# The first unit behind a norm in two narrow halves, one of them ahead of the norm's last turn; next weights requested earlier behind the mixers; a signal of their own for the convolution's taps

## The chip, the cores and the metric

The kernel runs on one core of one Trainium2 chip. The metric is the device time of one execution in microseconds. PE is the engine of the matrix products (TensorE), DVE is VectorE, ACT is ScalarE, POOL is GpSimd and SP is the engine that issues most of the DMAs (SyncE); SPq is SP's DMA issuing as the trace shows it. Kernels are compared by the median of runs that alternate on the same chip.

## What is computed

Two models in a row, batch 1, 512 tokens, width 1024, all in fp32. Their parts, cut to what matters here:

```python
def swiglu(h, w1, w3, w2):
    return (jax.nn.silu(h @ w1) * (h @ w3)) @ w2          # width of the hidden layer: 2816

def post_norm_residual(x, y, gate, weight, g, b):
    return layer_norm(ALPHA * x + weight * (1.0 + gate) * y, g, b)

def first_block(x, ...):                                   # 2 layers
    for l in range(DEPTH):
        h = x * (1.0 + scale[:, 0]) + shift[:, 0]
        x = post_norm_residual(x, swiglu(h, ...), gate[:, 0], 0.5, ...)
        h = x * (1.0 + scale[:, 1]) + shift[:, 1]
        x = post_norm_residual(x, hybrid_mixer(h, ...), gate[:, 1], 1.0, ...)
        h = x * (1.0 + scale[:, 2]) + shift[:, 2]
        x = post_norm_residual(x, swiglu(h, ...), gate[:, 2], 0.5, ...)

def hybrid_layer(x, ...):                                  # second model, 2 layers
    proj = rms_norm(x, norm1_g) @ w_in
    qkv = jax.nn.silu(causal_depthwise_conv(qkv, dn_conv_w))    # taps: 4 x 1536
    ...
    x = x + jnp.concatenate([o_dn, o_sc], axis=-1) @ w_out
    h2 = rms_norm(x, norm2_g)
    x = x + (jax.nn.silu(h2 @ ffn_w_gate) * (h2 @ ffn_w_up)) @ ffn_w_down
```

Every product of this program is a product of the normed and transposed h with a weight matrix that is read once from HBM.

## The kernel before

**Products.** An fp32 number is held as a high part (rounded to fp32r) and a low part (the rest). `product` (L159) makes one fp32 product of three matmuls: high x high (L163), low x high (L164), high x low (L165). Each matmul has a weight load of its own (PEld). ACT casts a weight to its high part, and DVE subtracts that from the weight to get the low part (`low_part`, L168). The weights come by DMA into two slots of `m_raw`. A "unit" is one tile of 128 output features over all 512 tokens: 8 slices k of the width 1024, 24 matmuls of 128x512. A 512-token tensor has 4 tiles of 128 tokens (TT is 4, DT is 8, HALF is 4).

**Stages.** The program is a row of stages, each opened by `stage` (L125), with a barrier of all engines between them (the profile names it by branches at L130). First model, twice: ffn0, proj1 and its attention stages, out1, ffn2. Second model, twice: proj2, delta, out2, ffn3. A stage's name ends in its layer: out1_0 is the output product of the first layer's mixer.

**The end of a stage with a norm.** `Down` (L494) makes the last product of an ffn or a mixer with the tokens on the partitions, 4 tiles in 8 banks of PSUM, row block by row block (`load_rows`, `high_act`, `low_dve`, `products`). While the last four row blocks are done tile by tile (`last_pe`, L572), ACT and DVE norm each finished tile (`norm_act` L627, `norm_dve` L721), PE turns the normed tile into columns (`turn_pe`, L593), and ACT and DVE make high and low parts of the turned tile (`high_norm`, `low_norm`). The norm of the last tile has nothing to hide behind but `keep_running` (L173): matmuls of a constant into an unused bank, which compute nothing. `filled` (L511) tells how many: 5 times two in a layer norm ("ln"), 3 times two in an rms norm ("rms"), and 7, with 12 more a tile earlier, where both follow each other ("ln_rms", the seam between the models).

**The start of the next stage.** `Ahead` (L103) requests the two first weight chunks of the next stage from the end of this one: ffn and mixer stages by `ahead.load(sp)`. `first_high_act` and `first_low_dve` (L110 to L116) split one slice k of the first chunk, 128x256, into `m_first_high` and `m_first_low` at the head of the norm. The next stage's PE starts with k = 0 on these, and goes on as the other 7 slices, 256 columns each, are split (`first_high`, `first_low`, L1107 to L1115, for the projections; the loops at the head of the scalar and vector blocks of `ffn`). The high and low parts of the second half (k of 4 and over) of the last tile are made in the next stage too: `carry_high` and `carry_low` (L480 to L490). In ffn, the two products of block f = 0 are made side by side, k by k.

**out1 and out2** (`mix_out`, L2215). 8 row blocks; SP requests blocks 4 to 7, waits until all 8 are split, and only then requests both slots of the next stage's weights. Everything of the norm waits for these weights, as the split stands at its head:

```python
            if ahead is not None:
                sp.wait_ge(S.rows_split, down.n)
                ahead.load(sp)
```

**proj2** (`mixer2_project`, L2344). POOL requests 11 small vectors, 4 of them the convolution's taps, all on one signal. DVE's first convolution step (L2373) waits for all 11, and behind it in DVE's order stands the low part of weight chunk 2.

**ffn's vectors.** `load_vectors` requests gate, shift, scale or gain ahead of the down product's rows, into room of their own.

Of the kernel before, what the change touches and what calls it, by code (L numbers as in the profile page):

```python
# [17 lines left out]
F32R = mybir.dt.float32r  # L18
# [80 lines left out]
class Memory:  # L99
    pass  # L100


class Ahead:  # L103


    def __init__(self, nc, tag, load, slots=2, first=None, count=0):
        self.landed = [nc.alloc_semaphore(f"{tag}_ahead{s}") for s in range(slots)]
        self.load = lambda sp: load(sp, self.landed)
        self.first, self.count = first, count

    def first_high_act(self, act, M):
        act.wait_ge(self.landed[0], self.count)
        high, _, raw = self.first(M)
        return act.copy(high, raw)

    def first_low_dve(self, dve, M):  # L116
        high, low, raw = self.first(M)
        return low_part(dve, low, raw, high)
# [375 lines left out]
class Down:  # L494
# [4 lines left out]
    def __init__(self, nc, memory, tag, M, I, boundary, w_down, raw, rows_high, rows_low, following, gate=None, gate_there=False, extra=0):  # L499
# [9 lines left out]
        self.vec = [sb(f"vec{n}", D) for n in range({"ln": 2, "ln_rms": 3, "rms": 1, "final": 1}[boundary.kind])]  # L509

        self.filled = {"ln": {TT - 1: 5}, "rms": {TT - 1: 3}, "ln_rms": {TT - 2: 12, TT - 1: 7}, "final": {}}[boundary.kind]  # L511
# [4 lines left out]
    def load_vectors(self, sp, S, gate_free=False):  # L516

        M, I, b = self.M, self.I, self.boundary
        if gate_free:
            sp.wait_ge(S.residual, 3 * TT)  # L520
        row = lambda ap: ap.partition_broadcast(P)
        if b.kind in ("ln", "ln_rms") and not self.gate_there:
            sp.dma_start(self.gate[:], row(M.mod_dram[b.layer, b.sub, 2])).then_inc(S.gate_landed, 16)
# [69 lines left out]
    def turn_pe(self, pe, S, i):  # L593
# [252 lines left out]
def ffn_first(M):  # L846
    two = lambda w: w[:].rearrange("p (w n) -> p w n", w=2)
    return two(M.first_high), two(M.first_low), M.raw[:, 0].rearrange("p (w k n) -> p w k n", w=2, k=DT)[:, :, 0]


def ffn_ahead(nc, M, tag, w_gate, w_up):
    return Ahead(nc, tag, lambda sp, landed: [ffn_load(sp, M, landed, w_gate, w_up, s, s) for s in range(2)], first=ffn_first, count=32)


def ffn(nc, M, I, tag, w_gate, w_up, w_down, boundary, mine, ahead=None, ada=None, residual=None, hid=None, carried=True):
# [5 lines left out]
    with ExitStack() as memory, stage(nc, tag, signals, mine) as (block, S):  # L861
# [9 lines left out]
                    ahead, res.g if res else None)  # L871
        down.rows_landed = [S.rows0_landed, S.rows1_landed, S.rows2_landed]
        down.ht = hid[:, 0:2 * TT, :].rearrange("p (i c) n -> p i (c n)", i=TT)
        done_first = 1 if carried else 0
# [7 lines left out]
        def _(sp):  # L882
            if res:
                res.load(sp, S)
            for f in range(2, FT):
                if f == 2:
                    sp.wait_ge(S.first_split, DT - done_first)
# [5 lines left out]
            down.load_vectors(sp, S, res is not None)  # L893
# [5 lines left out]
            for f in range(3, FT):  # L899
                down.load_rows(sp, S, f)  # L900
# [2188 lines left out]
```

## Time and profile before

| | us |
|---|---|
| median of 3 runs | 3656.82 (3651.94 to 3661.17) |
| the profiled execution's own time | 3657.5 |
| its span | 3655.7 |
| busy PE / DVE / ACT / POOL | 3561.3 / 1975.7 / 1227.5 / 150.9 |
| mean granted TensorE clock | 0.993 of full speed |

The profile is one execution on its one core. Its page gives the busy time of each engine; the timeline gives the start and length of each instruction, or of a group of equal ones, and in brackets the idle time before it with what ended it; the windows view gives busy time and the granted clock (PEclk, 1.00 is 2.4 GHz, 0.50 is 1.2 GHz) of a stretch. Matmuls are pipelined: a matmul of 128x512 lasts 0.39 us but the next starts after some 0.23 us, so the pace is read from the distance of starts. L numbers are lines of the kernel before.

### The profile page before, as it was taken

The page shows a single profiled execution, that of the slowest core. Times are in us where ns is not written, and L with a number is a line of the kernel's source. Part 1 is how long each engine was busy: PE and PEld are TensorE (multiplying, and loading weights), DVE is VectorE, ACT ScalarE, POOL GpSimd, SP SyncE. Part 2 cuts the span into 40 slices and gives each one's busy share as a digit, 9 for nine tenths or more (in the row PEclk, how much of TensorE's full clock was granted, in tenths as well). Part 3 has the DMA queues.
Part 4 walks back from the last instruction along what each step waited for, and adds up shares of the span by engine and source line. Part 5 has one row for each costly group of instructions (what it writes and reads, how often), then busy time and mean ns, then how long its engine had stood idle before and what let it go on. Part 6 is the DMA issues. An engine that isn't in the chain of part 4 may idle for free. (4 is left out here: it accounts for less than half of the span.)

```text
span 3655.7 us, 43309 instructions
## 1 busy us (share of the span) xinstructions
PE 3561.3 (97%) x17744; PEld 2933.0 (80%) x17744; DVE 1975.7 (54%) x3041; ACT 1227.5 (34%) x1928; POOL 150.9 (4%) x212
## 2 busy tenths in 40 slices
PE   7999999999999999999999999999999999999999
PEld 6888777678888888777678887788788878878887
DVE  6555665775456645665663355666322366553233
ACT  3222334532233222334532223635322355442222
POOL 1110100001000100100000001000000000000000
PEclk8999999999999999999999999999999999999999
DMA  7654331245433644331144331211334222113322
GB/s 268 230 184 128 83 102 41 71 154 190 143 128 110 219 161 128 83 96 47 55 131 126 106 136 48 79 38 53 92 94 126 98 48 75 41 53 104 104 98 81
DMA packets 438041, 397.74 MB, mean 109 GB/s; under 512 B 53779, under 2 KB 390275, under 8 KB 437844
## 3 DMA queue, kind: packets, MB, share of 16 engines
q1 hardware_dynamic: 413028, 310.53, 27.9%
q0 software_dynamic: 24816, 84.45, 6.8%
q8 instruction: 140, 2.29, 0.3%
q14 instruction: 57, 0.47, 0.0%
HBM read 390.14 MB, written 4.78 MB: 108 GB/s over the span
## 5 line engine op out<-in xcount | busy, mean ns | idle before, releaser
L163 PE MATMUL m_ps<-m_h_high,ffn_w_high 128*128 128x512 f32 x2100 | 821.7, 391 | 1.0 <-DVE ffn_w_low L170 1.0
L165 PE MATMUL m_ps<-m_h_high,ffn_w_low 128*128 128x512 f32 x2100 | 818.0, 390 | 0.0
L164 PE MATMUL m_ps<-m_h_low,ffn_w_high 128*128 128x512 f32 x2100 | 817.6, 389 | 0.0
L163 PEld LDWEIGHTS m_ps<-m_h_high,ffn_w_high 128*128 128x128 f32 x2100 | 394.8, 188 | 82.6 <-issue 1.1
L165 PEld LDWEIGHTS m_ps<-m_h_high,ffn_w_low 128*128 128x128 f32 x2100 | 394.5, 188 | 82.8
L164 PEld LDWEIGHTS m_ps<-m_h_low,ffn_w_high 128*128 128x128 f32 x2100 | 394.8, 188 | 81.3
L971 ACT ACTIVATE ffn_sil<-m_ps 128x512 f32<-128x512 f32 x132 | 79.1, 599 | 1128.9 <-PE m_ps L165 1128.9
L163 PE MATMUL m_ps<-ffn_w_high,ffn_hid_high 128*128 128x512 f32 x1056 | 411.6, 390 | 0.0
L165 PE MATMUL m_ps<-ffn_w_high,ffn_hid_low 128*128 128x512 f32 x1056 | 410.9, 389 | 0.0
L164 PE MATMUL m_ps<-ffn_w_low,ffn_hid_high 128*128 128x512 f32 x1056 | 410.9, 389 | 0.0
L1011 DVE TENSOR_TENSOR ffn_hid<-ffn_sil,m_ps 128x512 f32<-128x512 f32 x110 | 75.6, 687 | 549.7 <-ACT ffn_sil L971 549.6
L170 DVE TENSOR_TENSOR ffn_w_low<-m_raw,ffn_w_high 128x2048 fp32r<-128x2048 f32 (+1 forms) x168 | 303.7, 1823 | 112.4 <-ACT ffn_w_high L965 108.7
L170 DVE TENSOR_TENSOR ffn_w_low<-ffn_rows,ffn_w_high 128x1024 fp32r<-128x1024 f32 x132 | 161.6, 1224 | 291.5 <-ACT ffn_hid_high L979 291.4
L556 ACT CAST ffn_w_high<-ffn_rows 128x1024 fp32r<-128x1024 f32 x132 | 138.5, 1049 | 407.9 <-PE m_ps L165 395.4
L965 ACT CAST ffn_w_high<-m_raw 128x2048 fp32r<-128x2048 f32 x126 | 239.7, 1902 | 0.3 <-DMA m_raw<-in_ffn_w 0.2
L165 PEld LDWEIGHTS m_ps<-ffn_w_high,ffn_hid_low 128*128 128x128 f32 x1056 | 198.2, 188 | 41.2
L163 PEld LDWEIGHTS m_ps<-ffn_w_high,ffn_hid_high 128*128 128x128 f32 x1056 | 198.3, 188 | 41.1
L164 PEld LDWEIGHTS m_ps<-ffn_w_low,ffn_hid_high 128*128 128x128 f32 x1056 | 198.3, 188 | 40.5
L394 DVE SCALAR_TENSOR_TENSOR ffn_ada_part<-ffn_rows,m_ccol,ffn_ada_part 128x512 f32<-128x512 f32 x224 | 168.2, 751 | 86.8 <-DMA ffn_rows<-in_ada_w 78.8
L380 POOL DMA_DIRECT2D ffn_rows<-in_ada_w x128 | 91.2, 713 | 1475.0 <-issue 885.7
L163 PE MATMUL m_ps<-m_h_high,proj_w_high 128*128 128x512 f32 (+2 forms) x344 | 142.6, 415 | 3.5 <-DVE proj_w_low L170 3.5
L1535 ACT ACTIVATE attn_probs<-attn_probs,attn_shift 128x128 f32<-128x128 f32 (+3 forms) x128 | 71.0, 556 | 193.6 <-DVE attn_shift L1590 193.5
(485 smaller groups left out, 5439.3 us busy)
## 6 DMA issues: line engine op xcount, KB each, us to landing
m_raw<-in_ffn_w SPq DMA_DIRECT2D x176, 512.0 KB, 4.7
ffn_rows<-in_ada_w POOLq DMA_DIRECT2D x128, 512.0 KB, 5.0
ffn_rows<-in_ffn_w SPq DMA_DIRECT2D x88, 512.0 KB, 3.5
m_raw<-in_w_in SPq DMA_DIRECT2D x32, 1024.0 KB, 5.3
m_raw<-in_ffn_w_gate SPq DMA_DIRECT2D x44, 512.0 KB, 3.7
m_raw<-in_ffn_w_up SPq DMA_DIRECT2D x44, 512.0 KB, 4.8
ffn_rows<-in_ffn_w_down SPq DMA_DIRECT2D x44, 512.0 KB, 3.7
m_raw<-in_w_out SPq DMA_DIRECT2D x24, 512.0 KB, 4.7
```

What stands on the lines that cost most here:

```text
L163: pe.matmul(out, sh, mh, start=first, stop=False, skip_group_check=True)
L164: pe.matmul(out, sh, ml, start=False, stop=False, skip_group_check=True)
L165: return pe.matmul(out, sl, mh, start=False, stop=last, skip_group_check=True)
L170: return dve.tensor_tensor(low, value, high.bitcast(F32), ALU.subtract)
L380: queue.dma_start(self.slots[:, n % 2], src).then_inc([S.ada0_landed, S.ada1_landed][n % 2], 16)
L394: dve.scalar_tensor_tensor(out=part, in0=self.slots[:, n % 2, j, :], scalar=self.M.ccol[:, k + j:k + j + 1], in1=part, op0=ALU.mult, op1=A ...
L556: return act.copy(self.high[f % self.SLOTS], self.raw[f % self.raws])
L965: act.copy(w_high[:, f % 2], M.raw[:, f % 2]).then_inc(S.wide_high, 1)
L971: act.activation(sil[:, f % 2, :], M.ps[:, 2 * (f % 2), :], ACT.Silu).then_inc(S.silu_done, 1)
L1011: dve.tensor_tensor(hid[:, f, :], sil[:, f % 2, :], M.ps[:, 2 * (f % 2) + 1, :], ALU.mult).then_inc(S.hidden_done, 1)
L1535: ins = act.activation(probs(m, g), probs(m, g), ACT.Exp, bias=shift[:, m % 4, g:g + 1], accum_out=sums[:, p % 4, g, b:b + 1])
```

## The change

There are nine ends of a norm with a stage behind them: ffn0_0, out1_0, ffn2_0, ffn0_1, out1_1, ffn2_1, out2_0, ffn3_0 and out2_1. At each of them:

1. At the head of the norm, ACT and DVE split the whole first unit of the next stage (128 columns, all 8 slices k: 128x1024 each) into a new buffer `M.early`, where one slice of 256 columns was split before.
2. PE makes the first unit in two halves of 256 tokens (`half_pe`, 24 matmuls of 128x256 each). Half 0, of tokens 0 to 255, stands ahead of the last tile's turn, in place of that turn's `keep_running`. Half 1 is the next stage's first work. The 12 fillers of "ln_rms" a tile earlier stay.
3. The next stage begins with the carried parts of h on ACT and DVE, and splits the second 128 columns of chunk 0 in two pieces of four k. In ffn, bank 0 is now finished before bank 1 begins. ffn0_0, which has no norm ahead of it, makes both halves at its start, after its own split of 128x1024.

Further: 4. in `mix_out`, slot 0 of the next weights is requested once 6 of 8 row blocks are split, and slot 1 after 8. 5. In proj2, the 4 tap requests have a signal of their own; the first convolution step waits for them alone, and the others are waited for at a step much later (`gain`, n = 0). 6. In ffn, the gate is requested where all vectors were, and the rest behind row block 18 into spent rows of the hidden layer, which frees the room that `M.early` takes.

```diff
     def first_high_act(self, act, M):
         act.wait_ge(self.landed[0], self.count)
-        high, _, raw = self.first(M)
-        return act.copy(high, raw)
+        return act.copy(M.early[:, 0], self.first(M))
...
+    def half_pe(self, pe, M, half, S=None):
+
+        tokens = slice(2 * P * half, 2 * P * (half + 1))
+        for k in range(DT):
+            if S and k == HALF:
+                pe.wait_ge(S.carry_low, 2)
+            mm = product(pe, M.ps[:, 0, tokens], (M.early[:, 0, k], M.early[:, 1, k]), (M.h_high[:, k, tokens], M.h_low[:, k, tokens]),
+                         k == 0, k == DT - 1)
+        return mm
...
-        self.filled = {"ln": {TT - 1: 5}, "rms": {TT - 1: 3}, "ln_rms": {TT - 2: 12, TT - 1: 7}, "final": {}}[boundary.kind]
+        self.filled = {TT - 2: 12} if boundary.kind == "ln_rms" else {}
...
         if self.filled.get(i):
             pe.wait_ge(S.h_low, 1)
             keep_running(pe, self.M, 0, self.filled[i])
+        if i == TT - 1:
+            pe.wait_ge(S.next_low, 1)
+            pe.wait_ge(S.h_low, 2)
+            self.following.half_pe(pe, self.M, 0)
         pe.wait_ge(S.h_ready, i + 1)
...
             for f in range(3, FT):
                 down.load_rows(sp, S, f)
+                if f == SPENT_ROW:
+                    sp.wait_ge(S.rows_split, SPENT)
+                    down.load_vectors(sp, S)
...
                 if f == 0:
+                    if not carried:
+                        pe.wait_ge(S.first_split, 1)
+                        mine.half_pe(pe, M, 0)
+                    mine.half_pe(pe, M, 1, S if carried else None)
                     for k in range(DT):
-                        if k >= done_first:
-                            pe.wait_ge(S.first_split, k + 1 - done_first)
-                        if k == HALF and carried:
-                            pe.wait_ge(S.carry_low, 2)
-                        for which in range(2):
-                            w = (ffn_first(M)[0][:, which], ffn_first(M)[1][:, which]) if k == 0 else (high[:, which, k], low[:, which, k])
-                            mm = product(pe, bank(which), w, (M.h_high[:, k, :], M.h_low[:, k, :]), k == 0, k == DT - 1)
+                        if k % HALF == 0:
+                            pe.wait_ge(S.first_split, own_first + 1 + k // HALF)
+                        mm = product(pe, bank(1), (high[:, 1, k], low[:, 1, k]), (M.h_high[:, k, :], M.h_low[:, k, :]), k == 0, k == DT - 1)
...
-            if ahead is not None:
-                sp.wait_ge(S.rows_split, down.n)
-                ahead.load(sp)
+            for s in range(2):
+                sp.wait_ge(S.rows_split, down.n - 2 + 2 * s)
+                ahead.load(sp, s)
...
             if u == 0:
-                dve.wait_ge(S.others_landed, 16 * len(others))
+                dve.wait_ge(S.taps_landed, 16 * len(taps))
...
     def gain(n):
         def step(dve, S, link):
             half, i = n // TT, n % TT
+            if n == 0:
+                dve.wait_ge(S.others_landed, 16 * len(others))
```

How the instructions stand on PE at the end of ffn0_0 and the start of proj1_0, before (`m_tri,m_ident` are the fillers, L605 the turns):

```order
L605 MATMUL m_ps<-m_ident,m_hid 128x128 x7
L176 MATMUL m_ps<-m_tri,m_ident 128x256 [waits ffn0_0_h_low]
L176 MATMUL m_ps<-m_tri,m_ident 128x256 x4
L605 MATMUL m_ps<-m_ident,m_hid 128x128 [waits ffn0_0_h_ready]
L605 MATMUL m_ps<-m_ident,m_hid 128x128 x3
...
L1178 UNCONDITIONAL_BRANCH [waits barrier_Pool_Activation_PE_DVE_SP_release]
L163 MATMUL m_ps<-m_h_high,m_first_high 128x512
L164 MATMUL m_ps<-m_h_low,m_first_high 128x512
L165 MATMUL m_ps<-m_h_high,m_first_low 128x512
L163 MATMUL m_ps<-m_h_high,proj_0_w_high 128x512 [waits proj1_0_first_split]
```

And now:

```order
L624 MATMUL m_ps<-m_ident,m_hid 128x128 x7
L175 MATMUL m_ps<-m_h_high,m_early_first 128x256 [waits ffn0_0_h_low,ffn0_0_next_low]
L176 MATMUL m_ps<-m_h_low,m_early_first 128x256
L177 MATMUL m_ps<-m_h_high,m_early_first 128x256
...
L624 MATMUL m_ps<-m_ident,m_hid 128x128 [waits ffn0_0_h_ready]
L624 MATMUL m_ps<-m_ident,m_hid 128x128 x3
...
L1202 UNCONDITIONAL_BRANCH [waits barrier_Pool_Activation_PE_DVE_SP_release]
L175 MATMUL m_ps<-m_h_high,m_early_first 128x256
...
L175 MATMUL m_ps<-m_h_high,m_early_first 128x256 [waits proj1_0_carry_low]
...
L175 MATMUL m_ps<-m_h_high,proj_0_w_high 128x512 [waits proj1_0_first_split]
```

The fillers are gone. 24 matmuls of the next stage stand in their place, with waits for the split and for two low parts of the turned tile before; 24 more stand behind the barrier, 12 of them ahead of the wait for the carried low part, and the first wait for a piece of the new split comes after them all.

DVE at the start of proj1_0, before:

```order
L1215 UNCONDITIONAL_BRANCH [waits barrier_Pool_Activation_PE_DVE_SP_release]
L170 TENSOR_TENSOR proj_0_w_low<-m_raw,proj_0_w_high 128x256 [waits proj1_0_first_high] x3
L170 TENSOR_TENSOR m_h_low<-m_ps,m_h_high 128x4x128
L170 TENSOR_TENSOR m_h_low<-m_ps,m_h_high 128x4x128 [waits proj1_0_carry_high]
L170 TENSOR_TENSOR proj_0_w_low<-m_raw,proj_0_w_high 128x256 [waits proj1_0_first_high] x4
L170 TENSOR_TENSOR proj_0_w_low<-m_raw,proj_0_w_high 128x8x28 [waits proj1_0_w_high]
```

And now:

```order
L1239 UNCONDITIONAL_BRANCH [waits barrier_Pool_Activation_PE_DVE_SP_release]
L182 TENSOR_TENSOR m_h_low<-m_ps,m_h_high 128x4x128
L182 TENSOR_TENSOR m_h_low<-m_ps,m_h_high 128x4x128 [waits proj1_0_carry_high]
L182 TENSOR_TENSOR proj_0_w_low<-m_raw,proj_0_w_high 128x4x128 [waits proj1_0_first_high] x2
L182 TENSOR_TENSOR proj_0_w_low<-m_raw,proj_0_w_high 128x8x28 [waits proj1_0_w_high]
```

Seven pieces of the first chunk became two of half its width in all, and the carried low parts stand ahead of them.

## Rows read from the trace of the kernel before

**Rows 1.** The page: busy time of each engine over the span

```profile
PE 3561.3 (97%) x17744; PEld 2933.0 (80%) x17744; DVE 1975.7 (54%) x3041; ACT 1227.5 (34%) x1928; POOL 150.9 (4%) x212
```

**Rows 2.** Window view (columns: window, length, busy of each engine, PEclk, DMA share, GB/s)

```profile
776.00:1134.00 358.00, 357.11 (x1606) 296.52 (x1607) 196.06 (x214) 92.39 (x101) 22.81 (x32) 1.00 0.46 152
```

**Rows 3.** Timeline (start, us, engine, line, operation), norm at the end of ffn0_0

```profile
423.87 1.23 DVE L170 TENSOR_TENSOR m_h_low<-m_ps,m_h_high 128x1024 fp32r<-128x1024 f32 x1
...
426.23 2.32 PE L176 MATMUL m_ps<-m_tri,m_ident 128*128 128x256 f32 x10
...
429.30 0.42 PEld L605 LDWEIGHTS m_ps<-m_ident,m_hid 128*128 128x128 f32 x4 [1.15 <-DVE m_hid L757]
```

**Rows 4.** Timeline, wide and narrow products on PE, and a weight load

```profile
1163.54 0.39 PE L163 MATMUL m_ps<-m_h_high,ffn_w_high 128*128 128x512 f32 x1
...
1174.42 0.39 PE L163 MATMUL m_ps<-m_h_high,ffn_w_high 128*128 128x512 f32 x1
...
2345.08 0.28 PE L165 MATMUL m_ps<-proj_w_high,m_h_low 128*128 128x256 f32 x1
...
2345.44 0.19 PEld L163 LDWEIGHTS m_ps<-proj_w_high,m_h_high 128*128 128x128 f32 x1
...
2347.59 0.28 PE L165 MATMUL m_ps<-proj_w_high,m_h_low 128*128 128x256 f32 x1
```

**Rows 5.** Timeline, PE at the end of ffn3_0's norm (rms)

```profile
2955.15 1.46 PE L176 MATMUL m_ps<-m_tri,m_ident 128*128 128x256 f32 x6
...
2957.48 0.42 PEld L605 LDWEIGHTS m_ps<-m_ident,ffn_hid 128*128 128x128 f32 x4 [1.27 <-DVE ffn_hid L760]
```

**Rows 6.** Timeline, PE at the start of proj2_0

```profile
2261.97 0.40 PE L165 MATMUL m_ps<-m_h_high,m_first_low 128*128 128x512 f32 x1
...
2262.66 0.40 PE L164 MATMUL m_ps<-m_h_low,proj_w_high 128*128 128x512 f32 x1
```

**Rows 7.** Timeline, the split in front of ffn0_0's norm, and a cast of 1024

```profile
405.38 0.42 DVE L170 TENSOR_TENSOR m_first_low<-m_raw,m_first_high 128x256 fp32r<-128x256 f32 x1
...
407.54 1.22 DVE L709 CUSTOM_DVE_ANT_0 m_xr<-m_ps,m_xr 128x1024 f32<-128x1024 f32 x1 [1.74 <-PE m_ps L165]
...
745.97 1.05 ACT L556 CAST out_w_high<-m_raw 128x1024 fp32r<-128x1024 f32 x1 [4.39 <-PE m_ps L165]
```

**Rows 8.** Timeline, out1_0 from the sixth row's split to the first turn

```profile
737.07 1.22 DVE L170 TENSOR_TENSOR out_w_low<-m_raw,out_w_high 128x1024 fp32r<-128x1024 f32 x1
...
747.05 1.23 DVE L170 TENSOR_TENSOR out_w_low<-m_raw,out_w_high 128x1024 fp32r<-128x1024 f32 x1 [4.21 <-ACT out_w_high L556]
748.30 3.78 SPq L843 DMA_DIRECT2D m_raw<-in_ffn_w  x4
...
753.59 0.41 ACT L114 CAST m_first_high<-m_raw 128x256 fp32r<-128x256 f32 x1 [6.58 <-DMA m_raw<-in_ffn_w]
...
757.73 0.39 PE L165 MATMUL m_ps<-out_w_high,m_h_low 128*128 128x512 f32 x1
...
759.91 0.48 PE L163 MATMUL m_ps<-out_w_high,m_h_high 128*128 128x512 f32 x1
```

**Rows 9.** Timeline and one window, start of proj2_0

```profile
2263.18 4.05 POOL L1167 DMA_DIRECT2D b_conv_w<-in_dn_conv_w  x4 [244.37 <-issue]
...
2278.10 0.09 DVE L2373 MEMSET b_raw<- 128x36 f32 x1 [9.83 <-DMA b_norm_g<-in_dn_norm_g]
...
2284.73 2.28 DVE L170 TENSOR_TENSOR proj_w_low<-m_raw,proj_w_high 128x2048 fp32r<-128x2048 f32 x1
...
2287.07 0.28 PEld L163 LDWEIGHTS m_ps<-m_h_high,proj_w_high 128*128 128x128 f32 x1 [3.17 <-DVE proj_w_low L170]
...
2283.40:2305.00 21.60, 19.25 (x73) 14.39 (x72) 18.56 (x23) 12.74 (x15) 0.00 (x0) 0.92 0.32 98
```

**Rows 10.** Timeline at the start of ffn0_0, and a window in proj1_1

```profile
49.07 0.29 PEld L163 LDWEIGHTS m_ps<-m_h_high,m_first_high 128*128 128x128 f32 x1 [7.17 <-DVE m_first_low L170]
...
1529.00:1533.00 4.00, 4.00 (x12) 2.96 (x12) 3.82 (x10) 2.74 (x9) 0.00 (x0) 0.57 0.01 4
```

More of the change, by code:

```diff
@@ L846, in ffn_first @@
 def ffn_first(M):
-    two = lambda w: w[:].rearrange("p (w n) -> p w n", w=2)
-    return two(M.first_high), two(M.first_low), M.raw[:, 0].rearrange("p (w k n) -> p w k n", w=2, k=DT)[:, :, 0]
+    return M.raw[:, 0].rearrange("p (w k n) -> p w k n", w=2, k=DT)[:, 0]
+SPENT, SPENT_ROW = 14, 18
 def ffn_ahead(nc, M, tag, w_gate, w_up):
-    return Ahead(nc, tag, lambda sp, landed: [ffn_load(sp, M, landed, w_gate, w_up, s, s) for s in range(2)], first=ffn_first, count=32)
+    return Ahead(nc, tag, lambda sp, landed, *slots: [ffn_load(sp, M, landed, w_gate, w_up, s, s) for s in slots or range(2)], first=ffn_first, count=32)
 def ffn(nc, M, I, tag, w_gate, w_up, w_down, boundary, mine, ahead=None, ada=None, residual=None, hid=None, carried=True):
@@ L983, in _ @@
                 mine.first_high_act(act, M).then_inc(S.first_high, 1)
-            for k in range(1, DT):
-                if k == HALF and carried:
-                    carry_high(act, S, M)
-                act.copy(view(w_high, 0)[:, :, k], M.raw[:, 0].rearrange("p (w k n) -> p w k n", w=2, k=DT)[:, :, k]).then_inc(S.first_high, 1)
+            else:
+                carry_high(act, S, M)
+            for ks in first_pieces:
+                act.copy(view(w_high, 0)[:, 1, ks], view(M.raw, 0)[:, 1, ks]).then_inc(S.first_high, 1)
             split(1)
@@ L1027, in _ @@
                 mine.first_low_dve(dve, M).then_inc(S.first_split, 1)
-            for k in range(1, DT):
-                if k == HALF and carried:
-                    carry_low(dve, S, M)
-                dve.wait_ge(S.first_high, k + 1 - done_first)
-                low_part(dve, view(w_low, 0)[:, :, k], M.raw[:, 0].rearrange("p (w k n) -> p w k n", w=2, k=DT)[:, :, k],
-                         view(w_high, 0)[:, :, k]).then_inc(S.first_split, 1)
+            else:
+                carry_low(dve, S, M)
+            for n, ks in enumerate(first_pieces):
+                dve.wait_ge(S.first_high, own_first + n + 1)
+                low_part(dve, view(w_low, 0)[:, 1, ks], view(M.raw, 0)[:, 1, ks], view(w_high, 0)[:, 1, ks]).then_inc(S.first_split, 1)
             split(1)
@@ L1165, in _ @@
                     res.load(pool, S)
+                for dst, src in taps:
+                    pool.dma_start(dst, src).then_inc(S.taps_landed, 16)
                 for dst, src in others:
@@ L2487, in mixer2_project @@
     pe_steps.update({U + 2: turn_steps})
[L2488 removed]
+    project(nc, M, I, f"proj2_{l}", mixer2_chunks(I.w_in_2[l]), tiles, taps=taps, others=others, late_others=late_others, mine=mine, ahead=ahead,
             dve_steps=dve_steps, act_steps=act_steps, pe_steps=pe_steps, banks=4,
```

86 lines of the change are left out of this document (47 added, 39 removed).

## The prediction

> **What bounds the kernel now.** I read the page first: PE is busy for 3561.3 of 3655.7 us [rows 1]. Then the windows view inside an ffn: between 776 and 1134 PE is busy for 357.11 of 358.00 us at a clock of 1.00 [rows 2]. So neither DMA nor DVE sets the time there; only less work on PE, or an idle stretch of it filled, can move the end. Then the timeline of PE where the stages meet, since PE's busy time also holds work that serves nothing. At the end of ffn0_0 the last wide product is followed by turns, then ten filler matmuls from 426.23, and the last tile's turn starts at 429.30, when DVE has normed it [rows 3]. These 3.07 us are a latency of ACT and DVE, and the fillers only occupy PE. The change puts real work there at nine such seams.
>
> The sum is made against the profiled execution's own 3657.5 us, which lies 0.7 above the median of 3656.8.
>
> **Half units at nine seams.** The reader sees the price of a wide matmul in the distance of two starts: 48 matmuls of 128x512 in 1174.42 - 1163.54 = 10.88 us, 0.227 each, so a unit of 24 costs 5.45 us [rows 4]. The same three lines at 128x256 start 21 matmuls in 2347.59 - 2345.08 = 2.51 us, 0.120 each, although each has a weight load of 0.19 us beside it [rows 4]. A half is then 24 x 0.120 = 2.88 us. Before, a seam costs the window plus 5.45; now it costs the window, or 2.88 + 0.09 for the last matmul's end where that is longer, plus 2.88. In a layer norm the window is 3.07 [rows 3], so half 0 fits and the gain is 5.45 - 2.88 = 2.57 us. In an rms norm it is 2957.48 - 2955.15 = 2.33 [rows 5], so half 0 overshoots by some 0.6. Nine seams, three of them rms: 9 x 2.57 - 3 x 0.6 = 21.3 us. Half 0 needs tile 1's low part, which DVE ends at 423.87 + 1.23 = 425.10 [rows 3], ahead of 426.23, and the early split, long done.
>
> **Starts of stages.** Before, the pieces of the first split come late at some seams: at proj2_0 two neighbours start at 2261.97 and 2262.66, 0.69 apart instead of 0.23 [rows 6]. I summed such excesses at that start to 0.83 us, and in the same way at proj1_0 to 0.6, proj2_1 0.8, proj1_1 0.3 and ffn3_1 0.2, together 2.7. Now half 1 (2.88 us) runs on a finished split while ACT and DVE make the two pieces for unit 1. The new wait there, for the carried low part, stands behind 12 matmuls (1.44 us). Two parts of 512 at half the 1.23 us of a 1024 one [rows 3] give 1.2 and something for ACT's; that is close, and I cost it at 0 with 0.3 a seam as the upper end. I take the gain of 2.7 whole.
>
> **The larger split at the norm's head.** DVE's 256 columns took 0.42, then it idled 1.74 us for PE before its first norm step [rows 7]. The new low part of 1024 takes 1.23 [rows 3], the cast 1.05 [rows 7], against some 0.4 each: 0.8 us more on DVE and 0.65 more on ACT ahead of it. The 1.74 us cover that only if the DMA is early, as it is in an ffn; if the cover went, 1.4 us at the first turn would be the price. The ffn's moved vector loads only queue on SP behind 18 of 22 row blocks and are wanted at the norm: nothing.
>
> **out1 and out2.** Here the cover is missing: DVE ends the eighth split at 747.05 + 1.23, SP requests at 748.30, ACT casts at 753.59 after 6.58 us idle for that DMA, and the norm stands behind it. PE ends a tile at 757.73 and its next product starts at 759.91, so it lost 2.18 - 0.23 = 1.95 us at the first turn [rows 8]. The same reading gives 1.95 in out1_1, 0.77 in out2_0, 1.64 in out2_1: 6.3 us. Slot 0 now follows the sixth split, 737.07 + 1.23: 9.98 us earlier [rows 8]. Landing about 5.3 us after the request as before, it is there before the eighth split, and the longer split (1.4 us) leaves the norm some 4 us sooner than now. Bounds: nothing and 6.3; I take 6.3, since the distance is twice the loss.
>
> **proj2.** POOL issues the four taps from 2263.18 on, 4.05 us, and seven more requests after them; DVE's first step runs at 2278.10 after 9.83 us idle for the last vector; the low part of chunk 2 follows at 2284.73 for 2.28 us, and PE waits 3.17 us for it [rows 9]. The window 2283.40 to 2305.00, stall included, has PEclk 0.92 [rows 9]: 21.6 x 0.08 = 1.7 us of clock at most, of which I take 1.4, as some of it falls into the stall itself. With the taps alone, landing some 5 us after issue, DVE could go on near 2272 and chunk 2 would be ready 6 us sooner, against a PE that comes 2.6 sooner. The stall, 3.1 us, goes, its 1.4 us of clock too, and so does that of proj2_1, read in the same way as 1.6: 6.1 us. The bounds are 0 and 6.1. The seven others are now waited for many units later: nothing.
>
> **ffn0_0.** Its first product waits for DVE's low part until 49.07, 7.17 us idle [rows 10], and now for the larger split: 2.28 - 0.83 = 1.45 us later, and two halves are 0.31 dearer than a unit. Minus 1.7, once.
>
> **Sum.** 21.3 + 2.7 + 6.3 + 6.1 - 1.7 = 34.7 us: 3657.5 - 34.7 = 3622.8, on the median's scale 3622. A difference within 0.3% (11 us, so 3645.8 to 3667.8) is what a measurement of this kernel can't tell from no change.
>
> A rule that speaks against the halves: the Trainium skill, "TensorE: Matmul & The Clock Gate", Part 3, "The mechanism", says a weight load overlaps a running matmul only where the row groups differ; here all matmuls use the whole array. The trace disagrees for this shape: at 0.120 from start to start the loads of 0.19 can't stand in line with the matmuls [rows 4]. By the row the nine pairs of halves cost what is said above; by the rule they would turn the sum into a loss, which is rival 1 below.
>
> **The rivals.**
> 1. *Narrow matmuls are dear, their weight loads not hidden (slower).* The load of 0.19 is longer than the pace of 0.120 [rows 4]. The fillers are of the same shape, 128x256, and ten took 2.32 us, 0.232 each [rows 3]. If a half's matmuls go at that pace, it costs 5.57 us. A seam then costs 2 x 5.57 + 0.09 in place of the window and 5.45: 2.7 more in a layer norm, 3.4 in an rms norm, 9 x 2.71 + 3 x 0.74 = 26.6; ffn0_0 loses 5.69 + 1.45. Less the 15.1 us of stalls above, that is 18.6 us slower: 3676 on the execution's own scale, 3675 on the median's. It decides from a pace of about 0.19 us on. For it: the fillers. Against it: the fillers are of other type and helper, while the rows at 0.120 are the same helper's.
> 2. *The clock drops at the seams.* At proj1_1, and there alone of the seams, the window after the last turn has PEclk 0.57, 4.0 us that do 2.3 us of work: 1.7 lost [rows 10], at the 1.2 GHz level, after some 0.75 us of idleness ahead of the turn. If the missing fillers bring that to the eight others: 8 x 1.7 = 13.6, 3636. Against it: a half leaves PE as busy as the fillers did, the idle gap of a turn is not longer. The Trainium skill, same page, Part 1, ties the clock to TensorE's recent activity; by it the halves would count like the fillers, which no row here can show yet.
> 3. *The earlier weights don't help the mixers' ends*, since the norm there waits for another thing: 6.3 less, 3628.
> 4. *The gain is given back in the projections.* PE reaches chunk 2 2.6 us sooner after the start of the stage; where DVE's low part sets the pace, PE waits as long: 4 x 2.6 = 10.3, 3632. For it: the 3.17 us of rows 9 show how near DVE is.
> 5. *The change doesn't do what it says:* half 0 starts only when the norm is done, because its waits come late, and lies on the path. The windows stay as empty as before: 6 x 2.97 + 3 x 2.33 = 24.8 less, 3647, no difference. Against it are the 425.10 of rows 3 and the split at the norm's head.
>
> **The numbers.** My forecast has 0.60, rivals 2, 3 and 4 have 0.10, 0.12 and 0.09, rival 5 has 0.04, rival 1 0.03. What is left, 0.02, is a better outcome: the clock's drop at proj1_1 goes too. Faster: 0.93; same: 0.04; slower: 0.03. The likeliest is 3622. Its own range, from the median's spread of some 4 us and 9 x 0.3 of the carried wait, is 3616 to 3629; with rivals 2, 3 and 4 it reaches 3637, and 3613 below.
>
> **What would show it.** At the end of ffn0_0, 24 matmuls of 128x256 stand 0.12 apart between 426.2 and some 429.1, and the last turn starts 3.07 us after the first of them, 3.0 in ffn3_0. In out1_0, ACT's early cast has no DMA wait and the first turn's gap on PE is under 0.5 us. In proj2_0 the first convolution step comes before 2273 on the old scale, and PE has no idle second before chunk 2. Wrong would be a pace above 0.15, a turn that moves back by more than 0.7, a PEclk under 0.9 behind the other seams, or a wait of PE for DVE at chunk 2 of any projection.

## The result, and the profile after

| | before | changed |
|---|---|---|
| median of 3 runs, us | 3656.82 | 3624.79 (3619.05 to 3625.25) |
| ratio | | 0.9913, 95% interval 0.9900 to 0.9926 |
| span of the profiled execution | 3655.7 | 3622.9 |
| mean granted clock | 0.993 | 0.994 |

The change takes 32.0 us off, 0.87%. Measured again beside two later versions, the changed kernel had 3622.34 against 3655.21. One of those five executions took 14821.48 us, for which nothing here shows a cause; without it the median is 3621.96, and the ratios leave it out. The forecast was 3622.

The page's first row for the changed kernel; the row of before is [rows 1]:

```profile
PE 3536.6 (98%) x17902; PEld 2927.6 (81%) x17902; DVE 1972.7 (54%) x2991; ACT 1222.1 (34%) x1878; POOL 149.7 (4%) x212
```

PE is busy for 24.7 us less, and the span is 32.8 us shorter. So most of the gain is busy time that PE no longer has (half a unit now stands where the fillers stood), the rest is idleness that went. An ffn's inside is as before [rows 2]; windows view of the changed kernel (columns as there):

```profile
776.00:1120.00 344.00, 344.00 (x1554) 285.77 (x1553) 186.65 (x196) 87.07 (x89) 21.53 (x31) 1.00 0.48 157
```

**A seam of a layer norm.** Timeline of the changed kernel at the end of ffn0_1 (start, us, engine, line, operation), which answers to [rows 3]:

```profile
1515.15 0.36 PE L175 MATMUL m_ps<-m_h_high,m_early_out 128*128 128x256 f32 x1
...
1517.98 0.28 PE L177 MATMUL m_ps<-m_h_high,m_early_out 128*128 128x256 f32 x1
1518.27 0.42 PEld L624 LDWEIGHTS m_ps<-m_ident,ffn_hid 128*128 128x128 f32 x4 [0.22 <-DVE ffn_hid L776]
...
1520.57 0.19 PEld L175 LDWEIGHTS m_ps<-m_h_high,m_early_out 128*128 128x128 f32 x1 [1.21 <-issue]
...
1523.55 0.40 PE L175 MATMUL m_ps<-m_h_high,proj_w_high 128*128 128x512 f32 x1
```

Half 0's 24 matmuls begin 0.123 apart on average (1515.15 to 1517.98, 23 distances). The last turn follows 3.12 us after the first of them, where it stood 3.07 after the fillers' begin. The next stage's first weight load comes 2.30 behind the turn, as before, and unit 1 starts 2.98 later. No wait for carried parts or pieces is left in it.

**A seam of an rms norm**, the end of ffn3_0, which answers to [rows 5]:

```profile
2928.17 0.36 PE L175 MATMUL m_ps<-m_h_high,m_early_out 128*128 128x256 f32 x1
...
2931.03 0.90 PEld L624 LDWEIGHTS m_ps<-m_ident,ffn_hid 128*128 128x128 f32 x8
```

The turn comes 2.86 us after half 0's begin in place of 2.33, and has no wait of its own: half 0 is longer than this window by 0.53.

**A mixer's end**, out1_0, which answers to [rows 8]:

```profile
736.82 1.01 SPq L862 DMA_DIRECT2D m_raw<-in_ffn_w  x2
...
745.28 1.05 ACT L117 CAST m_early_out<-m_raw 128x1024 fp32r<-128x1024 f32 x1
...
749.83 1.22 DVE L728 CUSTOM_DVE_ANT_0 m_xr<-m_ps,m_xr 128x1024 f32<-128x1024 f32 x1 [2.06 <-PE m_ps L177]
...
756.09 0.39 PE L177 MATMUL m_ps<-out_w_high,m_h_low 128*128 128x512 f32 x1
756.32 1.03 PE L624 MATMUL m_ps<-m_ident,out_ht 128*128 128x128 f32 x8
757.11 0.48 PE L175 MATMUL m_ps<-out_w_high,m_h_high 128*128 128x512 f32 x1
```

The early cast waits for no DMA, DVE now waits for PE's product and not for weights, and the first turn has no gap. From product to product it is still 1.02 us: the turn's eight matmuls take that. The prediction took 0.23 off the 2.18 of before and called the rest a wait. The second turn of the same stage waits for nothing, and it shows what a turn costs; the last three rows are out2_0's first turn (kernel before):

```profile
766.60 0.40 PE L165 MATMUL m_ps<-out_w_high,m_h_low 128*128 128x512 f32 x1
766.83 1.04 PE L605 MATMUL m_ps<-m_ident,out_ht 128*128 128x128 f32 x8
767.63 0.48 PE L163 MATMUL m_ps<-out_w_high,m_h_high 128*128 128x512 f32 x1
...
2575.39 0.39 PE L165 MATMUL m_ps<-out_w_high,m_h_low 128*128 128x512 f32 x1
2576.39 1.09 PE L605 MATMUL m_ps<-m_ident,out_ht 128*128 128x128 f32 x8 [0.61 <-DVE out_ht L760]
2577.23 0.47 PE L163 MATMUL m_ps<-out_w_high,m_h_high 128*128 128x512 f32 x1
```

From product to product are 1.03 us there, so the wait in out1_0 was 2.18 - 1.02 = 1.16, and in out2_0 1.84 - 1.02 = 0.82.

**proj2.** The first convolution steps, PE's wait for chunk 2 in proj2_0, and DVE's low part and PE's gap in proj2_1, which answer to [rows 9]:

```profile
2255.86 0.09 DVE L2399 MEMSET b_raw<- 128x36 f32 x1 [5.45 <-DMA b_conv_w<-in_dn_conv_w]
...
2264.82 0.19 PEld L175 LDWEIGHTS m_ps<-m_h_high,proj_w_high 128*128 128x128 f32 x1 [0.66 <-DVE proj_w_low L182]
...
2945.71 0.09 DVE L2399 MEMSET b_raw<- 128x36 f32 x1 [6.59 <-DMA b_conv_w<-in_dn_conv_w]
...
2952.33 2.28 DVE L182 TENSOR_TENSOR proj_w_low<-m_raw,proj_w_high 128x2048 fp32r<-128x2048 f32 x1
...
2952.69 1.02 PE L2445 MATMUL m_ps<-b_sq,m_ones 128*128 128x512 f32 x2
2954.67 0.50 PE L175 MATMUL m_ps<-m_h_high,proj_w_high 128*128 128x512 f32 x1 [0.96 <-DVE proj_w_low L182]
2955.01 0.40 PE L176 MATMUL m_ps<-m_h_low,proj_w_high 128*128 128x512 f32 x1
```

In proj2_0 the wait of the weight load fell from 3.17 to 0.66 us, and hardly any of the 0.66 is lost to the matmuls. In proj2_1 the wait stayed. PE's rows at the same place in the kernel before:

```profile
2982.08 1.02 PE L2419 MATMUL m_ps<-b_sq,m_ones 128*128 128x512 f32 x2
...
2984.54 0.39 PE L164 MATMUL m_ps<-m_h_low,proj_w_high 128*128 128x512 f32 x1
```

From the first of the two sums to the second product of chunk 2 are 2.46 us before and 2.32 in the changed kernel. Where nothing waits it is 1.10 (experiment 8), so PE lost 1.4 us there and still loses 1.2.

**Where the time came from.** The same instruction of DVE or ACT, its start before minus its start after, place by place; what is gained between two of them is the place's gain. For instance DVE's first norm step of ffn2_0 and of ffn0_1, first in the kernel before, then in the changed one:

```profile
1127.77 1.23 DVE L709 CUSTOM_DVE_ANT_0 m_xr<-m_ps,m_xr 128x1024 f32<-128x1024 f32 x1 [1.73 <-PE m_ps L165]
...
1504.68 1.22 DVE L709 CUSTOM_DVE_ANT_0 m_xr<-m_ps,m_xr 128x1024 f32<-128x1024 f32 x1 [1.73 <-PE m_ps L165]
```

```profile
1122.24 1.22 DVE L728 CUSTOM_DVE_ANT_0 m_xr<-m_ps,m_xr 128x1024 f32<-128x1024 f32 x1 [0.93 <-PE m_ps L177]
...
1496.54 1.22 DVE L728 CUSTOM_DVE_ANT_0 m_xr<-m_ps,m_xr 128x1024 f32<-128x1024 f32 x1 [0.94 <-PE m_ps L177]
```

5.53 ahead of the seam behind ffn2_0, 8.14 after it: it gave 2.61. DVE's idleness ahead of its norm step also went from 1.73 to 0.93: the larger split took 0.8 of the cover, as costed, and nothing of the time.

| place | forecast | measured |
|---|---|---|
| start of ffn0_0 | -1.7 | -1.4 |
| seams behind ffn0_0 / out1_0 / ffn2_0 | 3.17 / 2.57 / 2.57 | 3.0 / 2.8 / 2.6 |
| seam behind ffn0_1 (the slow stretch of rows 10 is gone) | 2.87 | 4.2 |
| seam behind out1_1 | 2.57 | 2.8 |
| seam behind ffn2_1 with proj2_0 | 7.9 | 7.5 |
| seam behind out2_0 | 1.97 | 2.1 |
| seam behind ffn3_0 with proj2_1 | 4.37 | 2.6 |
| seam behind out2_1 | 2.17 | 2.1 |
| first turns of the four mixers' ends | 6.3 | 4.0 |
| unassigned, in the mixers | | 0.4 |
| sum | 34.7 | 32.7 |

What the starts of stages gave is part of the seams' places. There is one more row of the kernel before to be read with rows 6, the product that starts between the two that stand there:

```profile
2262.33 0.50 PE L163 MATMUL m_ps<-m_h_high,proj_w_high 128*128 128x512 f32 x1
```

### The profile page after: what moved, and what is told of

Its sections match the earlier page's. It is cut to its first block and busy times, and to the rows that moved or that the text cites. A ratio compares the mean times of both kernels' runs of the same rounds, so it can differ in the third digit from the quotient of the medians.

```text
span 3622.9 us, 43534 instructions
## 1 busy us (share of the span) xinstructions
PE 3536.6 (98%) x17902; PEld 2927.6 (81%) x17902; DVE 1972.7 (54%) x2991; ACT 1222.1 (34%) x1878; POOL 149.7 (4%) x212
## 3 DMA queue, kind: packets, MB, share of 16 engines
q8 instruction: 142, 2.33, 0.3%
## 5 line engine op out<-in xcount | busy, mean ns | idle before, releaser
L175 PE MATMUL m_ps<-m_h_high,ffn_w_high 128*128 128x512 f32 x2064 | 807.2, 391 | 0.6 <-DVE ffn_w_low L182 0.4
L177 PE MATMUL m_ps<-m_h_high,ffn_w_low 128*128 128x512 f32 x2064 | 803.5, 389 | 0.0
L176 PE MATMUL m_ps<-m_h_low,ffn_w_high 128*128 128x512 f32 x2064 | 803.1, 389 | 0.0
L182 DVE TENSOR_TENSOR ffn_w_low<-m_raw,ffn_w_high 128x2048 fp32r<-128x2048 f32 (+1 forms) x138 | 296.4, 2151 | 116.6 <-ACT ffn_w_high L990 116.6
L175 PE MATMUL m_ps<-m_h_high,proj_w_high 128*128 128x512 f32 (+2 forms) x320 | 131.3, 410 | 1.0 <-DVE proj_w_low L182 1.0
```

Of the source, the lines that this page charges most:

```text
L175: pe.matmul(out, sh, mh, start=first, stop=False, skip_group_check=True)
L176: pe.matmul(out, sh, ml, start=False, stop=False, skip_group_check=True)
L177: return pe.matmul(out, sl, mh, start=False, stop=last, skip_group_check=True)
L182: return dve.tensor_tensor(low, value, high.bitcast(F32), ALU.subtract)
```

## The experiments

Runs of one kernel lie some 4 to 14 us apart. The traces show one source: between 1740 and 1790 us, and between 650 and 700, inside a mixer, the granted clock falls in some executions and not in others. In the first of these windows it is 0.92 in the kernel before, 0.90 in the changed one and 1.00 when that was run again; in the second it is 0.90 in experiments 2, 3 and 9 and 0.93 to 1.00 in the others. It goes with no version of the kernel, and the profiles of before and after have it at the same place, so that it hardly shows in their difference. Differences of 1 or 2 us are therefore read from the traces place by place, and only larger ones from medians. The kernel before had 3653.97, 3654.01 and 3655.21 in the three sets.

### From the kernel before to the changed one in four steps

**1. Without halves.** Requests and taps of the change put into the kernel before:

```diff
-                sp.wait_ge(S.rows_split, down.n)
-                ahead.load(sp)
+            for s in range(2):
+                sp.wait_ge(S.rows_split, down.n - 2 + 2 * s)
+                ahead.load(sp, s)
...
-                dve.wait_ge(S.others_landed, 16 * len(others))
+                dve.wait_ge(S.taps_landed, 16 * len(taps))
```

> The kernel before with the earlier weight requests behind the mixers and the taps' own signal alone; no early split, no halves, fillers as before. Theory (the seams' halves carry most of the gain, and each part is worth what stands idle on PE in the trace before): the first turns of the four mixers' ends stop waiting, 1.15 + 1.15 + 0.85 + 0.85 = 4.0 us, and proj2 loses its stalls and slow stretch, 3.1 + 1.6 + 1.4 = 6.1: 3656.8 - 10.1 = 3646.7. Rival (the requests and taps carry most, since PE then meets the stages in another rhythm): 20 us or more faster, 3636 or less. Rival (they help only together with the halves): 3656.

3647.4, ratio 0.9979 (0.9969 to 0.9989): 7.7 us by the ratio, interval 4 to 11, which holds the theory's 10.1 and shuts out the rivals. All four first turns show 1.02 us from product to product, 4.0 us less in all, and PE goes through chunk 2 of both proj2 without a wait; place by place proj2_0 gives 4.1 us and proj2_1 1.4.

**2. The unit whole and wide.**

```diff
-        tokens = slice(2 * P * half, 2 * P * (half + 1))
+        if half == 0:
+            return
+        tokens = slice(0, T)
```

(with no call of it ahead of the last turn, and `filled` as before)

> The changed kernel with the first unit made whole and wide (24 matmuls of 128x512) at the start of the next stage, on the early split; fillers as in the kernel before. Against the run without halves, only the whole early split is new. Theory: stalls at the starts of stages go (2.7 us), the first stage starts 1.4 later: 1.3 faster than that run, 3645.4. Rival (the longer split at the norm's head isn't covered): 1.4 us at each of nine norms, 3658.

3648.25, ratio 0.9977 (0.9966 to 0.9987), the same as step 1 within its interval. That excludes a cost of 1.4 us at each norm, the rival; the theory's 1.3 is too small to be seen in the medians. Against step 1 this run also has the moved vector loads of ffn, the carried parts first and bank 0 finished before bank 1, so that it shows all of these together to cost nothing that can be seen.

**3. Both halves behind the barrier.**

```diff
                 if n == 0:
+                    mine.half_pe(pe, M, 0)
                     mm = mine.half_pe(pe, M, 1, S)
```

> As the one before, but the first unit as two halves of 128x256, both behind the barrier; fillers as in the kernel before. Theory: the narrow form costs 2 x 2.88 against 5.45, 0.31 more per seam, 3.1 in all with the first stage: 3648.5; and the changed kernel differs from this run only by where half 0 stands, 25 us. Rival (narrow matmuls at the fillers' pace of 0.232): 5.7 per unit, 3700.

3650.94, ratio 0.9990 (0.9980 to 0.9999). The medians put the narrow form at 2.7 us in all where 3.1 were expected; the intervals of the two runs overlap, so this shows only that it is small, and not the rival's 50. From here to the changed kernel (0.9913) is 0.77%, some 28 us, where 25 were expected: the gain is where half 0 stands. A part of the 28 can be the clock, as the next step shows.

**4. The window left empty.** As 3, without `keep_running` ahead of the last turns:

```diff
-        self.filled = {"ln": {TT - 1: 5}, "rms": {TT - 1: 3}, "ln_rms": {TT - 2: 12, TT - 1: 7}, "final": {}}[boundary.kind]
+        self.filled = {TT - 2: 12} if boundary.kind == "ln_rms" else {}
```

> As the one before, both halves behind the barrier, but nothing in the last turn's window: the fillers that kept PE running are left out there. Theory A (the window's idleness is too short to lower the clock): same as with fillers, 3648.5, PEclk 1.00 behind every seam. Theory B (the clock drops behind each seam, as the fillers are there to prevent): up to nine times the 1.7 us lost at proj1_1, 3664, with PEclk near 0.6 in the 4 us behind most of the last turns.

3662.92, 12.0 us slower than step 3: theory B. Windows of 8 us from the second matmul behind a seam (behind out1_0, ffn2_1 and out2_1), with the window empty:

```profile
778.85:786.85 8.00, 8.00 (x49) 8.00 (x49) 4.43 (x5) 4.33 (x5) 1.42 (x2) 0.67 0.93 283
2263.31:2271.31 8.00, 8.00 (x48) 8.00 (x48) 4.43 (x5) 3.05 (x4) 6.61 (x8) 0.65 0.60 122
3290.59:3298.59 8.00, 8.00 (x47) 8.00 (x47) 4.43 (x5) 4.33 (x5) 0.00 (x0) 0.64 0.58 173
```

and the same three, from the first matmul, with fillers (step 3):

```profile
782.44:790.44 8.00, 8.00 (x58) 7.63 (x59) 4.78 (x5) 4.68 (x5) 1.42 (x2) 1.00 0.87 273
2263.50:2271.50 8.00, 8.00 (x59) 7.59 (x59) 4.58 (x5) 3.80 (x5) 6.45 (x8) 1.00 0.60 124
3284.16:3292.16 8.00, 8.00 (x59) 7.59 (x59) 4.59 (x5) 4.50 (x5) 0.00 (x0) 1.00 0.57 170
```

With the window empty PE is idle for some 2.9 us (3.6 behind ffn2_1, 2.2 in the rms norms), runs its eight turning matmuls, idles again for up to 1.0 us at the barrier, and is at the 1.2 GHz level within 0.4 us of the next stage's start at all nine seams (PEclk 0.62 to 0.81 over the 8 us from the first matmul). The Trainium skill ("TensorE: Matmul & The Clock Gate", Part 1) ties the level to TensorE's recent activity, and the trace agrees. So half 0 has two offices: it is work, and it keeps PE running. It does the second better than the fillers. In the four kernels with fillers (before and steps 1 to 3), 7 of 36 seams show a drop; in the eight profiles with half 0 in the window, 3 of 72. By kind of seam: in the five layer norms 5 of 20 with fillers and 0 of 40 with half 0, in the three rms norms none of 12 and none of 24. The difference thus comes from the layer norms. The seam between the models, behind ffn2_1, shows none: 2 of 4 and 3 of 8. There half 0 ends before the window does and PE idles again, in all eight profiles alike (the last turn starts 0.97 us after half 0's last matmul), though the clock fell in three of them only. These rows are of the repeated run of the changed kernel:

```profile
2238.64 1.32 PE L624 MATMUL m_ps<-m_ident,ffn_hid 128*128 128x128 f32 x8 [0.69 <-DVE ffn_hid L793]
...
2241.15:2249.15 8.00, 8.00 (x41) 7.35 (x41) 4.59 (x5) 3.80 (x5) 6.45 (x8) 0.79 0.60 120
```

### Parts undone in the changed kernel

**5. Both requests behind the eighth split.**

```diff
-                sp.wait_ge(S.rows_split, down.n - 2 + 2 * s)
+                sp.wait_ge(S.rows_split, down.n)
```

> The changed kernel with both weight requests of the mixers' ends back behind the eighth split. Theory (the first turn's wait was 1.15 us in the layer norms, once the turn's own eight matmuls are taken off, and the larger split adds 1.4): loss at the first turn of out1_0 from 1.03 to some 3.6 us between products, in all 4.0 + 5.6 = 9.6 us slower than the changed kernel. Rival (the 1.95 of the prediction was the wait): 4.4 us between products, 11.9 in all. Rival (the norm waits for something else): no difference.

3637.68, ratio 0.9954 (0.9939 to 0.9969): 13 and 15 us above the changed kernel's two medians. The trace gives 4.2, 4.2, 2.7 and 3.9 us at the four mixers' ends, 15.0 in all. Timeline of PE at the first turn of out1_0, and behind it of out2_0:

```profile
756.98 0.39 PE L177 MATMUL m_ps<-out_w_high,m_h_low 128*128 128x512 f32 x1
759.74 1.57 PEld L624 LDWEIGHTS m_ps<-m_ident,out_ht 128*128 128x128 f32 x8 [2.79 <-DVE out_ht L776]
...
761.36 0.78 PE L175 MATMUL m_ps<-out_w_high,m_h_high 128*128 128x512 f32 x1
...
761.94 0.63 PE L176 MATMUL m_ps<-out_w_low,m_h_high 128*128 128x512 f32 x1
...
2559.26 1.09 PE L624 MATMUL m_ps<-m_ident,out_ht 128*128 128x128 f32 x8 [2.47 <-DVE out_ht L779]
2560.11 0.48 PE L175 MATMUL m_ps<-out_w_high,m_h_high 128*128 128x512 f32 x1
```

In out1_0 the turn starts 2.76 us after the last product, 0.23 of it the product's own: a wait of 2.5, which is the corrected 1.15 and the larger split's 1.4. What neither theory had is the rest: after this wait turns and products run at the lower clock (products 0.43 to 0.58 apart), 1.6 us more. The same happened in out1_1 and out2_1, after waits of 2.5 and 2.2 us; in out2_0 the wait was 2.6, the longest, and the clock stayed at 1.00. So the earlier requests are worth 4 us on the kernel before, and 15 with the larger split: without them almost half of the whole gain is lost.

**6. One wait for all eleven vectors.**

```diff
                 dve.wait_ge(S.taps_landed, 16 * len(taps))
+                dve.wait_ge(S.others_landed, 16 * len(others))
```

> The changed kernel, but the first convolution step of proj2 waits for all eleven small vectors again. Theory: DVE resumes some 4.6 us later (the seven other requests take POOL 4.6 us), PE waits before chunk 2 grow from 0.3 and 1.5 to about 5 and 6 us, 9 us slower with 1 to 3 us of a lower clock on top: 3634 to 3637. Rival (what the kernel before showed is what the taps are worth): 6.1, 3631.

3637.68 too, 0.9954 (0.9937 to 0.9970). The trace gives 7.3 us at proj2_0 and 6.0 at proj2_1, 13.3 in all. From the last product of chunk 1 to the second of chunk 2 are 6.99 and 6.31 us, where 1.32 are enough when nothing waits: PE loses 5.7 and 5.0 there, and then runs matmuls of 0.63 (the lower level) for a while. In proj2_0:

```profile
2263.56 0.09 DVE L2400 MEMSET b_raw<- 128x36 f32 x1 [10.75 <-DMA b_norm_g<-in_dn_norm_g]
...
2272.53 0.29 PEld L175 LDWEIGHTS m_ps<-m_h_high,proj_w_high 128*128 128x128 f32 x1 [4.07 <-DVE proj_w_low L182]
...
2273.12 0.63 PE L176 MATMUL m_ps<-m_h_low,proj_w_high 128*128 128x512 f32 x1
```

The taps too are worth more with the halves (13 us) than the 6.1 that the prediction read in the kernel before, or the 5.5 that step 1 gave, since PE now comes sooner to a DVE that is as late as ever.

### What was left, and how to have it

**7. Half 0 shortened in the rms norms, the rest behind the barrier.**

```diff
-            self.following.half_pe(pe, self.M, 0)
+            self.following.left = range(6, DT) if self.boundary.kind == "rms" else ()
+            self.following.half_pe(pe, self.M, 0, ks=range(DT - len(self.following.left)))
...
                 if n == 0:
+                    mine.half_pe(pe, M, 0, ks=mine.left)
                     mm = mine.half_pe(pe, M, 1, S)
```

> The changed kernel, but in the three rms norms only six of the eight slices k of half 0 stand in the window, and the last two behind the barrier. Theory (half 0 is longer than the rms window and pushes the last turn back): the last turn starts 2.35 us after half 0 began, not 2.95, six matmuls (0.72) more behind the barrier replace it: net 3 x -0.6 + 3 x 0.72, so nothing or 0.4 us slower, since the pushed part was work all the same. Rival (the overshoot is a loss of its own, for the stage's start waits for ACT and DVE behind the turn while PE idles): 18 matmuls fit, the turn is 0.6 earlier, and PE's idle part behind the turn is unchanged, so the 0.72 is paid at the start: again near 0. What tells: the sum of window, idle part and start in ffn3_0 against the changed kernel's.

3624.35: no difference, as expected.

**8. The low part of chunk 2 first.**

```diff
+                early = bool(taps) and c == 0
+                if early and n == last_tile[c]:
+                    W.round_low(dve, S, c + 2)
                 if dve_steps and n in dve_steps:
...
-                if n == last_tile[c] and c + 2 < len(chunks):
+                if not early and n == last_tile[c] and c + 2 < len(chunks):
```

> The changed kernel, but in proj2 DVE makes the low part of chunk 2 ahead of the second convolution step. Theory (what is left of PE's wait in proj2_1, 1.46 us, is DVE's order: landing of the taps, then two convolution steps, then the low part): the wait goes, and proj2_0's 0.3 too: 1.8 us faster. Rival (the convolution is then late for what stands behind it, the copies out of PSUM or the sums): the wait reappears at a later unit, no difference.

3620.81, 0.9909 (0.9894 to 0.9924), which the medians can't tell from the changed kernel. The trace can. proj2_1:

```profile
2948.82 2.28 DVE L182 TENSOR_TENSOR proj_w_low<-m_raw,proj_w_high 128x2048 fp32r<-128x2048 f32 x1
...
2952.14 1.02 PE L2448 MATMUL m_ps<-b_sq,m_ones 128*128 128x512 f32 x2
...
2953.24 0.40 PE L176 MATMUL m_ps<-m_h_low,proj_w_high 128*128 128x512 f32 x1
```

DVE makes the low part at 2948.82 in place of 2952.33, and from the first sum to the second product are 1.10 us in place of 2.32: the wait is gone, here and in proj2_0. Place by place proj2_1 gives 1.2 us and proj2_0 0.1, 1.3 where 1.8 were expected: the 1.5 and 0.3 of the expectation were again more than the place loses against one where nothing waits. The cause is settled: DVE's order behind late taps.

**9. The rest of half 0 behind the turn, ahead of the barrier.**

```diff
-            self.following.half_pe(pe, self.M, 0)
+            here = 6 if self.boundary.kind == "rms" else DT
+            self.following.half_pe(pe, self.M, 0, ks=range(here))
...
         mm.then_inc(S.turned, 1)
+        if i == TT - 1 and here < DT:
+            self.following.half_pe(pe, self.M, 0, ks=range(here, DT))
```

> The changed kernel, but in the three rms norms six of the eight slices k of half 0 stand ahead of the last turn and the last two right behind it, before the barrier. Theory (behind the turn PE idles some 1.5 us while ACT and DVE make the parts of the turned tile, so six matmuls of 0.72 us cost nothing there): the last turn is 0.6 us earlier at three seams, and the time from it to the next stage stays 2.46: 1.8 us faster than the changed kernel. Rival (the barrier then waits for PE): the 0.6 reappears between turn and stage, no difference.

3620.96 beside the changed kernel's 3622.34, which the medians can't tell apart. The trace can. The end of ffn3_0:

```profile
2931.73 0.36 PE L175 MATMUL m_ps<-m_h_high,m_early_out 128*128 128x256 f32 x1
...
2934.14 0.42 PEld L625 LDWEIGHTS m_ps<-m_ident,ffn_hid 128*128 128x128 f32 x4 [0.22 <-DVE ffn_hid L782]
...
2935.22 0.36 PE L175 MATMUL m_ps<-m_h_high,m_early_out 128*128 128x256 f32 x1
...
2936.44 0.19 PEld L175 LDWEIGHTS m_ps<-m_h_high,m_early_out 128*128 128x128 f32 x1 [0.48 <-issue]
```

The turn is back at 2.41 us after half 0's begin, six matmuls stand behind it, and the next stage's first load follows the turn by 2.30 as ever. Each of the three rms seams gives 0.5 us. The same comparison explains step 7: there too the turn came 0.5 earlier, but the six matmuls stood behind the barrier and took 6 x 0.120 = 0.72 us at the start.

**10. All of it.** 8 and 9, and ffn0_0's early split in four pieces of two slices, PE starting on the first (ACT and DVE likewise):

```diff
-                        pe.wait_ge(S.first_split, 1)
-                        mine.half_pe(pe, M, 0)
+                        for q in range(4):
+                            pe.wait_ge(S.first_split, q + 1)
+                            mine.half_pe(pe, M, 0, ks=range(2 * q, 2 * q + 2))
```

> The one before, with the low part of chunk 2 ahead of the second convolution step in proj2, and the first stage's early split in four pieces so that PE starts after the first. Theory: 1.8 of the seams, 1.8 of proj2 and 1.7 of the first stage, which starts 2.28 - 0.6 us sooner after its weights have landed: 5 us faster than the changed kernel, some 3619.5. Rival (the first stage waits for its next pieces or for chunk 1 whatever PE does): 3.6, 3621.

3618.35, ratio 0.9902 (0.9887 to 0.9916), against 3622.34 and 0.9907 (0.9891 to 0.9922) of the changed kernel, run beside it as

> The changed kernel once more, beside the two below on the same chip: 0.991 of the kernel before.

It is 4.0 us under it in the medians, near the 5 expected and within the intervals of both, so that it beats the kernel before is shown, and that it beats the changed one rests on the traces: PE's first load in ffn0_0 stands at 49.32 against 50.50 in the run beside it, the three seams give 1.5, proj2_1 1.4.

## Why the prediction was right, point by point

- **Half units: right in mechanism and size.** 0.123 from start to start where 0.120 was taken; layer norm seams 2.6 to 2.8 for 2.57, rms seams 2.1 for 2.0. (The 2.8 are behind out1_0 and out1_1, where the window before was 3.26 us long and not 3.07.) Rival 1, dear narrow matmuls, is out. So is, for this shape on this chip, the rule of the Trainium skill ("TensorE: Matmul & The Clock Gate", Part 3, "The mechanism") by which their loads would not be hidden. Rival 1's own price was a little high: ten fillers took 2.32 us with the last one's whole 0.38, so they start 0.216 apart, not 0.232.
- **Starts of stages: the wait went as forecast, its size was misread.** No start has a wait for a piece or for carried parts. But the two products of rows 6 are not neighbours: another one starts at 2262.33, between them, so that the 0.69 us hold two distances and only 0.23 of them were lost. Over the first 24 matmuls proj1_0, proj2_0 and proj2_1 each lost 0.5 us against the steady pace and the other starts at full clock some 0.1; half 1 still has that 0.1. That is 1.2 us in all where the prediction took 2.7.
- **The mixers' first turns: mis-sized.** The step "2.18 - 0.23 = 1.95 us" left out the turn's own eight matmuls. Measured is 1.16, 1.16, 0.82 and 0.85, 4.0 for 6.3. The same distance can be read at the turns that wait for nothing, where it is 1.02 or 1.03; it should have been the measure. And the 0.77 of out2_0 is not "the same reading": it is the distance to the turn (1.00) less 0.23, where the reading used for the others gives 1.84 - 0.23 = 1.61. The error would have been 0.8 larger without this slip.
- **proj2: right in proj2_0** (of the 7.9 with its seam 7.5), **wrong in proj2_1.** There "DVE could go on" some 5 us after the issue; the taps' wait ended at 2945.71, 6.7 after POOL had issued the last at 2938.98. Counted from PE's first load of the stage, that is 3.1 us sooner than before, and PE came to chunk 2 3.0 us sooner. So the wait hardly changed: 1.75 us of the term of 4.37 did not come.
- **The clock.** The drop of rows 10 did not come back, 1.3 us more; this had 0.02 as an outcome of its own. The four profiles with fillers have one to three drops, at different seams, so that the profile of before had one, and at proj1_1, was in part chance. The price of rival 2, 13.6 us for the seams, is close to the 12.0 that the empty window costs, but it is what the halves prevent.
- **Rivals 3, 4 and 5.** Rival 3 is out: with the early requests alone the four first turns wait for nothing (step 1), and both requests late cost 15 us. Rival 4 is true in a small way, at proj2_1 alone. Rival 5 is out, since half 0 starts right behind the turn ahead of it.
- **Nothing** was lost to the larger split at the norm's head, because the requests were moved too. On its own the term would have been wrong at the mixers' ends.
- **What was luck.** The sum came within 2.0 us of the measured 32.7 since the misses met. 2.3 too much at the mixers and 1.8 at proj2_1 stand against 1.3 too little at the seam of rows 10, and smaller ones both ways. And two of the prediction's own signs of being wrong appeared without moving the time much: PE waits for DVE at chunk 2 of proj2_1, and PEclk is 0.79 behind ffn2_1 in the repeated run.

## What to carry to other kernels

A window that only latency fills is best given real work that is ready by then, in a narrower form if need be, as long as the narrow form's pace is known from the trace. Ask what each part is worth after the others: earlier requests and the taps' signal were worth 4.0 and 5.5 us on the kernel before (step 1), 15 and 13 us in the changed one (experiments 5 and 6). And read a wait against the same place where nothing waits, not against zero.

## What the runs showed of the hardware

Waits of 2.2 to 2.5 us ahead of a turn brought PE to its lower level for the products behind them at three mixers' ends, and one of 2.6 us did not (experiment 5). Waits of 5.7 and 5.0 us did (experiment 6), while PE's idle 0.96 us in proj2_1 of the changed kernel did not. In the layer norms, fillers of 128x256 that took 2.32 of a 3.07 us window let the clock fall at 5 of 20 seams, and products of the same shape that filled the window at none of 40. Whether more fillers, up to the window's end, would have done as well was not tried. Matmuls of 128x256 with a weight load each start 0.120 us apart in the products (fp32r operands) and 0.216 in the fillers (fp32 constants); whether the type is the reason was not tried either.
